# The opening of a one-core encoder step: first norm and first two products rearranged

## Chip, cores and metric

The kernel runs on one core of a Trainium2 chip. TensorE (PE) multiplies, VectorE (DVE), ScalarE (ACT) and GpSimd (POOL) do the elementwise work, SyncE (SP) issues most transfers. The metric is the device time of one launch in microseconds (us).

## The reference, cut to what matters

The reference is one layer of a streaming encoder for 1024 prompt rows and 8 times 16 sample rows, 1152 rows of 1024 values in all. Only its first lines touch the change:

```
h = rmsnorm(x, norm_attn)                  # x * rsqrt(mean(x*x) + eps) * g
hq, hf, hi, hg, dq, dk, dv, mq, gl = split(h @ w_in)
fg = lb + (1 - lb) * sigmoid(hf)           # lb from a softmax over two rows of logits
k = 1 - fg;  b = cumsum(log(fg)) in chunks # HGRN2 branch, 8 heads of 128
bias = rel_bias[t5_bucket(pos_k - pos_q)]  # for the attention branch that comes second
```

After the HGRN2 branch come differential attention, attention to memory, a merge and a ConvFFN. They stay as they were.

## The kernel before, in words

Every product is made exact in three parts. ACT rounds a 128x1024 weight block to a high part (`round_w`, line 113), POOL subtracts for the low part (`rest_w`, line 118), and PE runs high times high, high times low and low times high. A product of one weight block (128 output features, all 1152 rows) is 8 slices of the inner dimension times 3 column groups of 384 rows times 3 parts, 72 matmuls of 128x384. A *piece* is one column group of it, 24 matmuls (`gemm_piece`). Weight blocks land in two staging buffers by turns; a load waits until the block two before has its low part.

PSUM is used as two groups of four banks. `take`, `ready` and `freed` hand a group from PE to the engine that reads it and back by counting semaphores, in a fixed order of results.

Each phase is one block of five instruction streams, one for each engine. All engines meet at the end of a block: nothing of the next block starts before every stream of this one is through.

`norm_phase` (line 199) works over nine tiles of 128 rows. For a tile, ACT squares and sums (line 256), POOL makes the reciprocal root (lines 328 and 329), DVE scales the rows (line 298), PE transposes them in 8 transposes (line 340), DVE multiplies by the gain into `h_full` (line 313), ACT rounds to `h_hi_part` (line 274) and DVE subtracts for `h_lo_part` (line 304). The row tile `x_rows` has four places. Beside tiles 0 and 1 PE makes the relative bias rows of all eight heads, four at a time, in banks 2 and 3 of both groups (line 349), and ACT copies them out (line 266) and stores them. The low parts of the first two weight blocks (forget, query) come last on POOL.

`hgrn_phase` (line 394) opens with both first products, forget and query, in full (line 892). Its SP stream loads the next two weight blocks, two mask constants, 18 pieces of the bias tables and four more constants (lines 468 to 485), the last of them `hgrn_onorm`. DVE waits for all of these constants at line 628. It adds the masks to the bias tables (lines 631 and 634, `near` and `bs`), and SP stores the tables in eight transfers (lines 517 to 522) before it loads the gate weight of head 0 (line 492). Then DVE does `decays` (key, forget gate, scan of the logarithm, first differences, lines 663 to 651) and `opening` (line 702), and enters the loop over heads. In a head, PE computes the score matrices DIAG, L0, L1, then the transposes VT, then L2 and so on. In front of each of them it takes a PSUM group and runs one *rider*, a piece of a product that is wanted later. DVE frees the group after the scores have been masked (line 698) and the rider copied (line 700). The rider of DIAG needs the low part of the value weight, rounded by ACT at line 544. VT waits until the scores of L1 are masked (line 839).

Of the kernel before, what the change touches and what calls it, by code (L numbers as in the profile page):

```python
# [14 lines left out]
P = 128  # L15
# [53 lines left out]
class Program:  # L69
# [12 lines left out]
    def setup(self):  # L82
# [13 lines left out]
        self.consts, self.cb = self.sem("constants_in"), 0  # L96
        self.dve = Count(nc.vector, self.sem("dve_chain"))
# [101 lines left out]
def norm_phase(g):  # L199

    nc = g.nc
    ctx = ExitStack()
    NX = 4
    xr = g.sb("x_rows", [P, NX, D], ctx=ctx)
# [7 lines left out]
    landed = [g.sem(f"x_landed{n}") for n in range(NX)]  # L212
    consts_in, cb = g.consts, g.cb
    summed, rstd, scaled, h_hi, h_lo, lb_sub, lb_exp = (
        g.sem(n) for n in ("x_summed", "x_rstd_ready", "x_scaled", "h_hi", "h_lo", "lb_shifted",
                           "lb_exp"))
    base_s = g.sem("base_constants")
# [4 lines left out]
    g.brow_out = g.sem("bias_row_out")  # L222

# [4 lines left out]
    with nc.Block() as block:  # L228
        @block.sync
        def _(sp):  # L230
            sp.dma_start(xr[:, 0, :], x_rows(0)).then_inc(landed[0], 16)
            sp.dma_start(g.ident[:], g.c["ident"]).then_inc(consts_in, 16)
            with nc.allow_non_contiguous_dma(reason="columns of 1024 values"):
                sp.dma_start(gcol[:], columns(g.x["norm_attn"][0])).then_inc(consts_in, 16)
                for n in range(2):
                    sp.dma_start(lbl[:, n, :], columns(g.x["hgrn_lb_logits"][n])).then_inc(consts_in, 16)
            sp.dma_start(table[:], g.x["rel_bias"]).then_inc(bias_in, 16)
            sp.dma_start(hot[:], g.c["bucket_hot"]).then_inc(bias_in, 16)
            for t in range(1, NT):
                if t >= NX:  # L240
                    sp.wait_ge(g.full, g.r + t - NX + 1)
                sp.dma_start(xr[:, t % NX, :], x_rows(t)).then_inc(landed[t % NX], 16)
                if t == NX - 1:
                    g.load_w(sp, g.w_in(W_HF), 0)
                    g.load_w(sp, g.w_in(W_HQ), 1)

        @block.scalar
        def _(act):
            act.wait_ge(base_s, 3)
            act.wait_ge(lb_sub, 3)  # L250
            act.activation(lbl[:], lbl[:], ACT.Exp).then_inc(lb_exp, 1)
            def squares(t):
                act.wait_ge(landed[t % NX], 16 * (t // NX + 1))
                if t:
                    act.wait_ge(summed, t)
                act.activation(sq[:], xr[:, t % NX, :], ACT.Square, accum_out=ss[:, t:t + 1]).then_inc(summed, 1)
            squares(0)
            squares(1)
            for t in range(NT):
                if t + 2 < NT:  # L260
                    squares(t + 2)
                if t in (0, 1):
                    act.wait_ge(brow_full, t + 1)
                    for n in range(2):
# [9 lines left out]
                act.activation(g.hhi[:, :, t * P:(t + 1) * P], tmp[:, t % 2], ACT.Copy).then_inc(h_hi, 1)  # L274

        @block.vector
        def _(dve):
# [5 lines left out]
            dve.wait_ge(consts_in, cb + 64)  # L283
# [11 lines left out]
            def scale(t):  # L295
                v = rs[:, t:t + 1]
                dve.wait_ge(rstd, t + 1)
                dve.tensor_scalar(xr[:, t % NX, :], xr[:, t % NX, :], v, None, ALU.mult).then_inc(scaled, 1)

            def rest(t):  # L300

                dve.wait_ge(h_hi, t + 1)
                cols = slice(t * P, (t + 1) * P)
                dve.tensor_tensor(g.hlo[:, :, cols], tmp[:, t % 2], g.hhi[:, :, cols].bitcast(F32), ALU.subtract)\
                    .then_inc(h_lo, 1)
            scale(0)
            for t in range(NT):
                if t + 1 < NT:
                    scale(t + 1)
                if t >= 2:  # L310
                    dve.wait_ge(h_lo, t - 1)
                ps = g.ready(dve, t)
                g.freed(dve.tensor_tensor(tmp[:, t % 2], ps[:, 0:2, :].rearrange("p c (k n) -> p (c k) n", n=P),
                                          gcol[:].unsqueeze(2).to_broadcast([P, KT, P]), ALU.mult), t)
                if t:
                    rest(t - 1)
            rest(NT - 1)

        @block.gpsimd
        def _(pool):  # L320
            pool.wait_ge(base_s, 3)
            pool.wait_ge(bias_in, 32)
            pool.tensor_scalar(spread[:], table[:].unsqueeze(2).to_broadcast([BUCKETS, HEADS, P]), 1.0, None, ALU.mult)\
                .then_inc(base_s, 1)
# [5 lines left out]
            g.rest_w(pool, 0)  # L330
            g.rest_w(pool, 1)

        @block.tensor
        def _(pe):
            pe.wait_ge(consts_in, cb + 64)
            for t in range(NT):
                pe.wait_ge(scaled, t + 1)
                ps = g.take(pe, t)
                for k in range(KT):
                    last = pe.transpose(ps[:, k // 4, (k % 4) * P:(k % 4 + 1) * P],  # L340
                                        xr[:, t % NX, k * P:(k + 1) * P], g.ident[:])
                last.then_inc(g.full, 1)
                if t in (0, 1):
                    if t:
                        pe.wait_ge(brow_r, 2)
                    else:
                        pe.wait_ge(base_s, 4)
                    for n in range(4):
                        last = pe.matmul(g.psum[n // 2][:, 2 + n % 2, 0:NREL], spread[:, 4 * t + n, :], hot[:],
                                         start=True, stop=True)  # L350
                    last.then_inc(brow_full, 1)
    g.cb += 64
# [41 lines left out]
def hgrn_phase(g):  # L394
# [8 lines left out]
    g.first = ExitStack()  # L403
    g.first_q, g.first_k = (g.sb(n, [P, ROWS], ctx=g.first) for n in ("diff_q", "diff_k"))
# [22 lines left out]
     ns_r, sq_r, rt_r, y1_r, y_r, ln_r, zero_r) = (g.sem(n) for n in (  # L427
# [3 lines left out]
         "sample_states_new", "out_squares_ready", "out_rstd", "out_normed", "y0_ready", "out_log", "hgrn_zeroed"))  # L431
# [9 lines left out]
    pre = Results(g, ["F", "Q"])  # L441
    g.r += pre.n
# [22 lines left out]
    with nc.Block() as block:  # L465
        @block.sync
        def _(sp):
            g.load_w(sp, g.w_in(W_HI), W_VT)
            g.load_w(sp, g.w_in(W_HG), W_GS)
            sp.dma_start(chid, g.c["chunk_hidden"]).then_inc(consts_in, 16)  # L470
# [3 lines left out]
            sp.wait_ge(g.brow_out, 16)  # L474
# [56 lines left out]
        def _(act):  # L531
            act.wait_ge(zero_r, 1)
# [88 lines left out]
        def _(dve):  # L621
            dve.memset(sc[:], 0.0).then_inc(zero_r, 1)
# [132 lines left out]
            with dve.Fori(0, HEADS - 1) as i:  # L755
                head(i)
# [1922 lines left out]
```

## Time and profile before

| what | us |
|---|---|
| median of 3 runs | 3357.67 |
| lowest, highest | 3355.53, 3358.48 |
| the profiled execution's own time | 3354.4 |
| its span | 3352.6 |
| PE busy | 3149.6 (94%) |
| DVE, ACT, POOL busy | 1388.4, 1127.4, 872.6 |

The span runs from the first to the last instruction of the core. The profiled execution lies below the three timed runs, by 3.3 us against their median. Busy time of PE counts pipelined matmuls and does not say how fast they are; their spacing does.

### The profile page before, as it was taken

What the parts mean: (1) busy time and instruction counts of PE and PEld (TensorE: products, weight loads), DVE (VectorE), ACT (ScalarE), POOL (GpSimd) and SP (SyncE); (2) the same over time, 40 slices, a digit from 0 to 9 for tenths busy, and PEclk for the clock granted to TensorE, in tenths of its full rate; (3) what the DMA queues carried; (4) which work ended last, traced back from release to release, by engine and by line L of the source; (5) the groups of instructions that cost most, each with busy time, mean ns of one, the idle gap of its engine ahead of it and who ended that gap; (6) DMA issues with size and microseconds to landing.
All of it is one profiled execution on the core that took longest, in us unless ns stands there. A gap on an engine that the chain in (4) does not pass through costs nothing. (4 is left out here: it accounts for less than half of the span.)

```text
span 3352.6 us, 50047 instructions
## 1 busy us (share of the span) xinstructions
PE 3149.6 (94%) x19550; PEld 2963.1 (88%) x19550; DVE 1388.4 (41%) x1446; ACT 1127.4 (34%) x1586; POOL 872.6 (26%) x520
## 2 busy tenths in 40 slices
PE   6999999999999999999688888999979999999997
PEld 5899999999988888888477778999979999999996
DVE  5554354443525555555532322222044444444443
ACT  3344333433334444444332221112242222222222
POOL 2333233332312111212002121243343323222230
PEclk9999999999999999999799999999989999999998
DMA  5212121121258777877665536432211111111101
GB/s 158 70 40 72 52 59 56 49 72 52 59 105 149 120 134 139 158 131 146 124 132 141 122 101 215 142 108 73 79 38 57 38 44 44 38 44 38 38 25 68
DMA packets 684752, 295.69 MB, mean 88 GB/s; under 512 B 350524, under 2 KB 665436, under 8 KB 684680
## 3 DMA queue, kind: packets, MB, share of 16 engines
q1 hardware_dynamic: 680232, 285.90, 35.6%
q10 hardware_dynamic: 4448, 8.80, 0.7%
q8 instruction: 49, 0.80, 0.1%
q14 instruction: 23, 0.19, 0.0%
HBM read 240.23 MB, written 54.41 MB: 88 GB/s over the span
## 5 line engine op out<-in xcount | busy, mean ns | idle before, releaser
L118 POOL TENSOR_TENSOR weight_lo<-weight_stage,weight_hi 128x1024 fp32r<-128x1024 f32 x180 | 453.0, 2518 | 1480.5 <-ACT weight_hi L113 1480.5
L1862 PE MATMUL group<-act_hi_part,weight_hi 128*128 128x384 f32 x1056 | 360.8, 342 | 13.6 <-DVE act_lo_part L2091 9.3
L1863 PE MATMUL group<-act_lo_part,weight_hi 128*128 128x384 f32 x1056 | 359.8, 341 | 0.0
L1864 PE MATMUL group<-act_hi_part,weight_lo 128*128 128x384 f32 x1056 | 359.7, 341 | 0.0
L165 PE MATMUL group<-h_hi_part,weight_hi 128*128 128x384 f32 x936 | 332.9, 356 | 27.6 <-DVE key_rows L700 20.1
L113 ACT ACTIVATE weight_hi<-weight_stage 128x1024 fp32r<-128x1024 f32 x180 | 190.6, 1060 | 422.5 <-PE group L2133 231.9
L166 PE MATMUL group<-h_lo_part,weight_hi 128*128 128x384 f32 x936 | 318.8, 341 | 0.0
L167 PE MATMUL group<-h_hi_part,weight_lo 128*128 128x384 f32 x936 | 318.4, 340 | 0.0
L2131 PE MATMUL group<-act_hi_part,weight_hi 128*128 128x384 f32 x768 | 259.4, 338 | 12.1 <-DVE act_lo_part L2044 12.1
L2132 PE MATMUL group<-act_lo_part,weight_hi 128*128 128x384 f32 x768 | 258.6, 337 | 0.0
L2133 PE MATMUL group<-act_hi_part,weight_lo 128*128 128x384 f32 x768 | 258.5, 337 | 0.0
L1350 PE MATMUL group<-h_hi_part,weight_hi 128*128 128x384 f32 x696 | 244.0, 351 | 1.1 <-ACT next_v L1096 1.0
L1350 PE MATMUL group<-h_hi_part,weight_lo 128*128 128x384 f32 x696 | 237.8, 342 | 0.0
L1350 PE MATMUL group<-h_lo_part,weight_hi 128*128 128x384 f32 x696 | 235.9, 339 | 0.0
L698 DVE COPY_PREDICATED scores<-level_masks,group 128x1152 f32<-128x1152 uint32 (+2 forms) x88 | 91.8, 1073 | 308.8 <-PE group L823 307.7
L1862 PEld LDWEIGHTS group<-act_hi_part,weight_hi 128*128 128x128 f32 x1056 | 199.6, 189 | 17.1 <-issue 9.9
L165 PEld LDWEIGHTS group<-h_hi_part,weight_hi 128*128 128x128 f32 x936 | 179.5, 192 | 35.7 <-issue 20.5
L1863 PEld LDWEIGHTS group<-act_lo_part,weight_hi 128*128 128x128 f32 x1056 | 199.7, 189 | 0.0
L1864 PEld LDWEIGHTS group<-act_hi_part,weight_lo 128*128 128x128 f32 x1056 | 199.6, 189 | 0.0
L166 PEld LDWEIGHTS group<-h_lo_part,weight_hi 128*128 128x128 f32 x936 | 179.2, 191 | 4.3 <-issue 3.3
L167 PEld LDWEIGHTS group<-h_hi_part,weight_lo 128*128 128x128 f32 x936 | 179.1, 191 | 0.0
L2408 DVE TENSOR_TENSOR residual<-residual,group 128x1152 f32<-128x1152 f32 x80 | 108.4, 1354 | 163.2 <-PE group L2523 163.2
(348 smaller groups left out, 6691.3 us busy)
## 6 DMA issues: line engine op xcount, KB each, us to landing
weight_stage<-in_w_in SPq DMA_DIRECT2D x88, 512.0 KB, 4.8
cached_v<-in_cache_diff_v SPq DMA_DIRECT2D x128, 256.0 KB, 5.1
cached_k<-in_cache_diff_k SPq DMA_DIRECT2D x224, 128.0 KB, 4.3
weight_stage<-in_w_up SPq DMA_DIRECT2D x44, 512.0 KB, 3.9
y_stage<-scratch_y_branch SPq DMA_DIRECT2D x24, 576.0 KB, 9.4
gate_in<-scratch_gates SPq DMA_DIRECT2D x24, 576.0 KB, 3.8
weight_stage<-in_w_branch SPq DMA_DIRECT2D x24, 512.0 KB, 3.9
down_stage<-in_w_down SPq DMA_DIRECT2D x22, 512.0 KB, 3.6
```

The costliest lines, as they stand in the source:

```text
L113: act.activation(self.whi[:, n % 2, :], self.wst[:, n % 2, :], ACT.Copy).then_inc(self.w_hi, 1)
L118: pool.tensor_tensor(self.wlo[:, n % 2, :], self.wst[:, n % 2, :], self.whi[:, n % 2, :].bitcast(F32), ALU.subtract).then_inc(self.w_lo, 1)
L165: pe.matmul(out, wh[:, k, :], xh[:, k, cols], start=(k == 0), stop=False)
L166: pe.matmul(out, wh[:, k, :], xl[:, k, cols], start=False, stop=False)
L167: last = pe.matmul(out, wl[:, k, :], xh[:, k, cols], start=False, stop=(k == KT - 1))
L1350: ins = pe.matmul(rider_bank, w[:, k, :], x[:, k, c * CW:(c + 1) * CW], start=(at == 0), stop=(at == STEPS - 1))
L1862: pe.matmul(o, w[0][:, k, :], ahi[:, k, rows], start=(k == 0), stop=False)
L1863: pe.matmul(o, w[0][:, k, :], alo[:, k, rows], start=False, stop=False)
L1864: last = pe.matmul(o, w[1][:, k, :], ahi[:, k, rows], start=False, stop=(k == KT - 1))
L2131: pe.matmul(o, wh[:, k, :], ahi[:, k, cols], start=(k == 0 and open_sum), stop=False)
L2132: pe.matmul(o, wh[:, k, :], alo[:, k, cols], start=False, stop=False)
L2133: last = pe.matmul(o, wl[:, k, :], ahi[:, k, cols], start=False, stop=(k == KT - 1))
```

## The change

In the norm, every tile gets its own place in `x_rows`, so a load waits for a square sum and no more for a transposition. The lower bound of the forget gate is computed at the end instead of the beginning. Bias rows are made one head at a time, one matmul behind each tile from tile 2 on. POOL makes the low parts of tiles 1, 3, 5 and 7, DVE the others. The two first products are cut into six pieces; five of them are run by PE inside the norm's block, in bank 3 of each group: forget 0 behind tile 5, query 0 behind tile 7, then forget 1, query 1 and forget 2 after the last bias row. ACT copies each out (through the sigmoid for forget). The sixth, query 2, opens `hgrn_phase`. In that phase the wait for the stored bias rows moves in front of the two mask loads, and DVE adds the masks to the bias tables after `opening` and no more before `decays`. In `diff_phase` the rider semaphores are replaced by the two of the pieces, counted on; several semaphores of zeroed buffers are one.

```diff
 # norm_phase
-    NX = 4
-    xr = g.sb("x_rows", [P, NX, D], ctx=ctx)
+    xr = g.sb("x_rows", [P, NT, D], ctx=ctx)
+    g.piece_bank = [g.psum[n][:, 3, 0:CW] for n in range(2)]
+    pieces = [(p, c) for c in range(NC) for p in range(2)]
+    def bias_bank(h):
+        return g.psum[(g.r + h + 1) % 2][:, 2, 0:NREL]
 # sync: x0, ident, x1, norm_attn, x2, w(HF), x3, rel_bias, bucket_hot, w(HQ), x4..x8, lb_logits
+            def load_x(t):
+                if t >= 4:
+                    sp.wait_ge(summed, t - 3)
+                sp.dma_start(xr[:, t, :], x_rows(t)).then_inc(landed[t % 4], 16)
 # scalar
-            act.wait_ge(lb_sub, 3)
-            act.activation(lbl[:], lbl[:], ACT.Exp).then_inc(lb_exp, 1)
             squares(0)
             squares(1)
             for t in range(NT):
                 if t + 2 < NT:
                     squares(t + 2)
                 if t in (0, 1):
-                    act.wait_ge(brow_full, t + 1)
-                    for n in range(2):
-                        h = 4 * t + 2 * n
-                        act.activation(brow[:, h:h + 2, :], g.psum[n][:, 2:4, 0:NREL], ACT.Copy).then_inc(brow_r, 1)
-                if t == 1:
-                    act.wait_ge(brow_r, 4)
-                    act.dma_start(g.s["bias_row"].rearrange("h p n -> p h n"), brow[:]).then_inc(g.brow_out, 16)
-                if t == 3:
-                    g.round_w(act, 0)
-                    g.round_w(act, 1)
+                    g.round_w(act, t)
+                if t >= 3:
+                    bias_row(t - 3)
+                if t == 7:
+                    piece_out(0)
                 act.wait_ge(g.free[(g.r + t) % 2], (g.r + t) // 2 + 2)
                 act.activation(g.hhi[:, :, t * P:(t + 1) * P], tmp[:, t % 2], ACT.Copy).then_inc(h_hi, 1)
+            bias_row(HEADS - 2)
+            piece_out(1)
+            bias_row(HEADS - 1)
...
+            piece_out(2)
+            piece_out(3)
+            piece_out(4)
 # vector: rest(t) now for even t only; the lower bound's six operations after rest(NT - 1)
 # gpsimd
             for t in range(NT):
...
+                if t == 1:
+                    pool.wait_ge(bias_in, 32)
+                    pool.tensor_scalar(spread[:], ...)
+                if t in (2, 3):
+                    g.rest_w(pool, t - 2)
+                if t in (3, 5, 7):
+                    rest(t - 2)
+            rest(NT - 2)
 # tensor
+            def piece(k):
+                p, c = pieces[k]
+                w = g.w_parts(pe, p)
+                pe.wait_ge(h_lo[0], (2, 3, 5)[c])
+                pe.wait_ge(h_lo[1], (1, 3, 4)[c])
+                if c:
+                    pe.wait_ge(g.piece_out, k - 1)
+                g.gemm_piece(pe, g.piece_bank[p], w, (g.hhi, g.hlo), c).then_inc(g.piece_full, 1)
             for t in range(NT):
...
+                if 2 <= t:
+                    bias_row(t - 2)
+                if t == 5:
+                    piece(0)
+                if t == 7:
+                    piece(1)
+            bias_row(HEADS - 1)
+            piece(2)
+            piece(3)
+            piece(4)
 # hgrn_phase, sync
             g.load_w(sp, g.w_in(W_HI), W_VT)
             g.load_w(sp, g.w_in(W_HG), W_GS)
+            sp.wait_ge(g.brow_out, 16)
             sp.dma_start(chid, g.c["chunk_hidden"]).then_inc(consts_in, 16)
...
-            sp.wait_ge(g.brow_out, 16)
 # hgrn_phase, scalar
-            ps = pre.ready(act, "F")
-            pre.freed(act.activation(tiles(fg[:]), ps[:, 0:NC, 0:CW], ACT.Sigmoid), "F")
             act.wait_ge(fg_r, 1)
             act.activation(fg[:], fg[:], ACT.Ln).then_inc(logf_r, 1)
+            act.wait_ge(g.piece_full, 6)
+            act.activation(qq[:, 2 * CW:], g.piece_bank[1], ACT.Copy).then_inc(g.piece_out, 1)
             g.round_w(act, W_VT)
-            ps = pre.ready(act, "Q")
-            pre.freed(act.activation(tiles(qq[:]), ps[:, 0:NC, 0:CW], ACT.Copy), "Q")
 # hgrn_phase, vector
             dve.wait_ge(consts_in, cb + 96)
-            dve.wait_ge(near_in, NEAR_IN)
-            (the two and the four additions of masks to the bias tables)
...
             decays(0, 0)
             opening(0, 0)
+            dve.wait_ge(near_in, NEAR_IN)
+            (the same six additions)
 # hgrn_phase, tensor
-            for n, j in (("F", 0), ("Q", 1)):
-                w = g.w_parts(pe, j)
-                g.gemm_t(pe, pre.take(pe, n), w, (g.hhi, g.hlo)).then_inc(g.full, 1)
-            pre.wait_freed(pe, "Q")
+            w = g.w_parts(pe, 1)
+            pe.wait_ge(g.piece_out, 4)
+            g.gemm_piece(pe, g.piece_bank[1], w, (g.hhi, g.hlo), 2).then_inc(g.piece_full, 1)
+            pe.wait_ge(g.piece_out, 6)
```

## Rows read from the trace of the kernel before

**Rows 1.** Page, part 1: busy us (share of the span) of each engine.

```profile
PE 3149.6 (94%) x19550; PEld 2963.1 (88%) x19550; DVE 1388.4 (41%) x1446; ACT 1127.4 (34%) x1586; POOL 872.6 (26%) x520
```

**Rows 2.** Waits of SP's queue, first 130 us: total, times, longest.

```profile
SPq L228 <- PEq L228: 19.2, 1, 19.2
```

**Rows 3.** Timeline, PE in the norm: start, duration, instruction, idle before.

```profile
14.20 5.48 PE L349 MATMUL group<-bucket_hot,bias_table_spread 32*128 32x384 f32 x8
...
32.89 1.97 PE L340 MATMUL group<-ident,x_rows 128*128 128x128 f32 x8 [2.29 <-DVE x_rows L298]
...
35.82 1.97 PE L340 MATMUL group<-ident,x_rows 128*128 128x128 f32 x8 [0.96 <-DVE x_rows L298]
```

**Rows 4.** Timeline, ACT and POOL at the start of the norm.

```profile
7.11 1.28 ACT L251 ACT_TABLE_LOAD   x1 [7.11 <-DVE lb_logits L288]
...
7.67 2.77 POOL L323 TENSOR_SCALAR bias_table_spread<-bias_table 32x1024 f32<-32x1024 f32 x1 [7.23 <-DMA bucket_hot<-in_bucket_hot]
```

**Rows 5.** Timeline, DVE and POOL at the norm's end.

```profile
43.64 6.02 POOL L118 TENSOR_TENSOR weight_lo<-weight_stage,weight_hi 128x1024 fp32r<-128x1024 f32 x2
44.61 2.83 DVE L298 TENSOR_SCALAR x_rows<-x_rows,x_rstd 128x1024 f32<-128x1024 f32 x1
47.36 1.21 DVE L313 TENSOR_TENSOR h_full<-group,norm_attn_col 128x1024 f32<-128x1024 f32 x1
...
48.49 2.25 DVE L304 TENSOR_TENSOR h_lo_part<-h_full,h_hi_part 128x1024 fp32r<-128x1024 f32 x1
```

**Rows 6.** Timeline, POOL: a low part with no DVE work beside it.

```profile
139.19 2.35 POOL L118 TENSOR_TENSOR weight_lo<-weight_stage,weight_hi 128x1024 fp32r<-128x1024 f32 x1
```

**Rows 7.** Windows: length; busy (count) of PE, PEld, DVE, ACT, POOL; clock; DMA; GB/s.

```profile
54.80:59.40 4.60, 4.58 (x14) 4.60 (x15) 1.16 (x2) 0.00 (x0) 0.00 (x0) 1.00 0.80 226
59.40:80.00 20.60, 20.60 (x120) 20.60 (x120) 6.02 (x8) 3.70 (x3) 0.00 (x0) 1.00 0.67 175
```

**Rows 8.** Timeline, PE: riders of DIAG and L1, scores of L1, rider and transposes of VT.

```profile
86.85 0.69 PE L165 MATMUL group<-h_hi_part,weight_hi 128*128 128x384 f32 x1 [4.69 <-POOL weight_lo L118]
...
103.07 0.44 PE L165 MATMUL group<-h_hi_part,weight_hi 128*128 128x384 f32 x1 [2.09 <-DVE key_rows L700]
...
108.91 2.17 PE L823 MATMUL group<-mixed 128*128 128x128 f32 x18
...
113.36 0.44 PE L165 MATMUL group<-h_hi_part,weight_hi 128*128 128x384 f32 x1 [2.27 <-DVE key_rows L700]
...
119.20 1.15 PE L184 MATMUL group<-ident,key_rows 128*128 128x128 f32 x9
```

**Rows 9.** Timeline, SP from the barrier on, and DVE behind it.

```profile
54.63 1.00 SPq L107 DMA_DIRECT2D weight_stage<-in_w_in  x2
...
69.20 0.43 SPq L485 DMA_DIRECT2D hgrn_onorm<-in_hgrn_onorm  x1
...
73.77 2.49 DVE L631 TENSOR_TENSOR gate<-gate,out_squares 128x1024 f32<-128x1024 f32 x2 [17.66 <-DMA hgrn_onorm<-in_hgrn_onorm]
```

**Rows 10.** Timeline, DVE and ACT, from `decays` to the scores of L1.

```profile
79.08 0.87 DVE L663 TENSOR_SCALAR key<-diff_q,bound_less_one,one_less_bound 128x1152 f32<-128x1152 f32 x1
...
80.91 1.17 ACT L543 ACTIVATE diff_q<-diff_q 128x1152 f32<-128x1152 f32 x1 [7.42 <-DVE diff_q L665]
...
82.11 2.56 DVE L667 TENSOR_TENSOR_SCAN log_decay<-scan_keep,diff_q 128x1152 f32<-128x1152 f32 x1 [1.23 <-ACT diff_q L543]
...
103.16 1.46 DVE L698 COPY_PREDICATED scores<-level_masks,group 128x1152 f32<-128x1152 uint32 x1 [0.15 <-DVE key_rows L700]
...
104.97 0.75 DVE L678 TENSOR_TENSOR mixed<-decay,diff_k 128x576 f32<-128x576 f32 x1
...
111.33 1.46 DVE L698 COPY_PREDICATED scores<-level_masks,group 128x1152 f32<-128x1152 uint32 x1 [3.14 <-PE group L823]
```

**Rows 11.** Timeline, first table load behind the barrier, and SP behind the tables.

```profile
69.76 1.28 ACT L541 ACT_TABLE_LOAD   x1 [16.66 <-PE group L152]
...
88.14 9.29 SPq L107 DMA_DIRECT2D weight_stage<-in_w_in  x2
```

More of the change, by code:

```diff
@@ L282, in _, with scale, rest @@
             dve.sem_inc(g.free[1], 1)
-            dve.wait_ge(consts_in, cb + 64)
+            dve.wait_ge(consts_in, cb + 32)
+            def scale(t):
+                v = rs[:, t:t + 1]
+                dve.wait_ge(rstd, t + 1)
+                dve.tensor_scalar(xr[:, t, :], xr[:, t, :], v, None, ALU.mult).then_inc(scaled, 1)
+            def rest(t):
+                dve.wait_ge(h_hi, t + 1)
+                cols = slice(t * P, (t + 1) * P)
+                dve.tensor_tensor(g.hlo[:, :, cols], tmp[:, 0], g.hhi[:, :, cols].bitcast(F32), ALU.subtract)\
+                    .then_inc(h_lo[0], 1)
+            scale(0)
+            for t in range(NT):
+                if t + 1 < NT:
+                    scale(t + 1)
+                if t >= 2:
+                    dve.wait_ge(h_lo[t % 2], t // 2)
+                ps = g.ready(dve, t)
+                g.freed(dve.tensor_tensor(tmp[:, t % 2], ps[:, 0:2, :].rearrange("p c (k n) -> p (c k) n", n=P),
+                                          gcol[:].unsqueeze(2).to_broadcast([P, KT, P]), ALU.mult), t)
+                if t % 2:
+                    rest(t - 1)
+            rest(NT - 1)
+            dve.wait_ge(lb_in, 32)
             dve.tensor_tensor(lbm[:], lbl[:, 0, :], lbl[:, 1, :], ALU.max).then_inc(lb_sub, 1)
@@ L294, in _, with rest @@
             g.dve.done(dve.tensor_scalar(g.lb1n[:], g.lb1[:], -1.0, None, ALU.mult))
[L295 to L317, printed above, removed]
         @block.gpsimd
         def _(pool):
+            def rest(t):
+                pool.wait_ge(h_hi, t + 1)
+                cols = slice(t * P, (t + 1) * P)
+                pool.tensor_tensor(g.hlo[:, :, cols], tmp[:, 1], g.hhi[:, :, cols].bitcast(F32), ALU.subtract)\
+                    .then_inc(h_lo[1], 1)
             pool.wait_ge(base_s, 3)
-            pool.wait_ge(bias_in, 32)
-            pool.tensor_scalar(spread[:], table[:].unsqueeze(2).to_broadcast([BUCKETS, HEADS, P]), 1.0, None, ALU.mult)\
-                .then_inc(base_s, 1)
             for t in range(NT):
@@ L340, in _ @@
                     last = pe.transpose(ps[:, k // 4, (k % 4) * P:(k % 4 + 1) * P],
-                                        xr[:, t % NX, k * P:(k + 1) * P], g.ident[:])
+                                        xr[:, t, k * P:(k + 1) * P], g.ident[:])
                 last.then_inc(g.full, 1)
[L343 to L352, printed above, removed]
+                if 2 <= t:
[8 more added lines that the diff above has]
+            piece(4)
+    g.cb += 32
     g.r += NT
@@ L754, in _ @@
             opening(0, 0)
+            dve.wait_ge(near_in, NEAR_IN)
+            for n in range(2):
+                g.dve.done(dve.tensor_tensor(near[n], near[n], chid.unsqueeze(1).to_broadcast([P, 4, 2 * P]), ALU.add))
+            for n in range(2):
+                for k in range(2):
+                    ins = dve.tensor_tensor(
+                        bs[k][:, :, n, :].rearrange("p h (b s) -> p h b s", s=DEC_S),
+                        toep[:, 4 * k:4 * k + 4, :].unsqueeze(2).to_broadcast([P, 4, DEC_B, DEC_S]),
+                        shid[:, n, :].rearrange("p (b s) -> p b s", s=DEC_S).unsqueeze(1)
+                        .to_broadcast([P, 4, DEC_B, DEC_S]), ALU.add)
+                    if (n, k) == (1, 1):
+                        ins.then_inc(near_r, 1)
+                    else:
+                        g.dve.done(ins)
             with dve.Fori(0, HEADS - 1) as i:
@@ L1346, in ride @@
                         if at == 0:
-                            pe.wait_ge(rider_free, rider(piece, i, last) + 1)
+                            pe.wait_ge(g.piece_out, rider(piece, i, last))
                         k, part = divmod(at, 3)
```

119 lines of the change are left out of this document (62 added, 57 removed).

## The prediction

> **What bounds the kernel now.** I read the page's first part, then the waits and the timelines of the first 130 us, since nothing behind them changes. PE is busy for 94% of the span [rows 1], so over the whole kernel a microsecond by which the heads' loop starts later is a microsecond at the end. The opening is different: there PE waits for others. The waits show SP standing 19.2 us at a block's border [rows 2]: engines that are through with the norm wait until all are. The border is passed at 54.63, when SP issues its next loads [rows 9]. Behind it PE runs 144 matmuls of the two first products, the first 14 at 0.33 us each and the next 120 at 0.172 [rows 7]. Meanwhile DVE waits 17.7 us for the last of 24 transfers that SP could issue only after the border: 54.63 to 73.77 [rows 9]. From 73.77 the end is set by DVE, not by PE: masks on the bias tables until 79.08, then `decays` and `opening` until about 103 [rows 10]. PE stands still for 4.7 us before the rider of DIAG, and 2.1 and 2.3 us before those of L1 and VT, each time behind DVE or what DVE holds up [rows 8]. After the scores of L1 PE leads again: its next matmul, the rider of VT, starts at 113.36 [rows 8]. I call this point S. The prediction is where S goes, and what happens to the border on the way.
>
> **Part 1: from the border B to S.** Before, S is B + 58.7 (113.36 less 54.63). After, the chain is:
> - B to the last constant: SP issues the same transfers in the same order; the wait for the stored bias rows is only moved up by two small loads, and their store is issued about 12 us ahead of B. 19.1 us.
> - `decays` may start at once, since the masks come later: key and gate, 79.08 to 80.91 [rows 10], 1.8 us.
> - The logarithm is now ACT's first operation behind the border. The first one of a stage has its table load behind its waits (7.11, and 69.76) [rows 4, 11]. 1.3 us, or 0 if the load slips in front of the wait. I take 1.3, since both first operations show it.
> - Logarithm, 1.2 us; from the scan's start at 82.11 to the point where the scores of L0 begin at 103.16, 21.05 us [rows 10]. ACT rounds the value weight behind this logarithm, as before, so POOL's low part holds up DVE's differences again at the same place.
> - The masks on the tables, now here: 73.77 to 79.08, 5.3 us [rows 9, 10].
> - Scores of L0 until DVE is ready for L1: 103.16 to 108.19 (111.33 less 3.14), 5.0 us. Scores of L1 until S, 111.33 to 113.36, 2.0 us [rows 8, 10].
>
> Sum 56.8 us. PE's own branch is shorter: it may start the rider of L1 at B + 44.4 and needs 8.0 us to the end of the L1 matrices (103.07 to 111.08) [rows 8], so B + 52.4, while DVE comes to the scores of L1 at B + 54.8. So the moved masks cost 2.4 us of path, not 5.3, and 1.9 us are saved against 58.7. That is all that can be won behind the border. PE, freed of five sixths of its products there, waits: query 2 is done at about B + 5, and the low part of the value weight, rounded behind the logarithm, comes 4.7 us after the scan's start (86.85 less 82.11), at B + 28. Some 23 us of PE stand empty. Bounds of this part: 55.5 (no table load) to 57.5.
>
> **Part 2: where the border goes.** First the norm up to piece 0. The first square no longer waits for the lower bound. With some 5 us for the first tile to land, table load, square, root and scaling, the first transposes start near 9. Then POOL and DVE get in each other's way. At 44.61 a scaling took 2.83 us while POOL made a low part; it ended 0.8 us after the first of POOL's two must have ended. The low part at 48.49 took 2.25 and ended 1.1 after POOL's second. `h_full`, which reads PSUM, took its 1.21 beside POOL [rows 5]. So I count scalings (0.75) and DVE's low parts (1.1) as excluded while POOL runs a large operation. Before the transposes of tile 5, that adds up to: spreading the table 2.8 [rows 4], two weight and two tile low parts on POOL at 2.35 [rows 6], five scalings, and two low parts on DVE: 2.8 + 9.4 + 3.75 + 2.2 = 18.1 us. Laid one behind the other from 9.3, with some 3.5 us in which this port is idle because the next user waits for a transposition, `h_full` or the rounding, the transposes of tiles 1 to 5 start at 12.8, 16.0, 21.5, 25.5 and 31.1. With their 2 us and a bias row of 1.3 (5.48 for what four heads take, two records each, so 1.28) [rows 3], piece 0 starts at 34. Without any exclusion the same layout gives 28.8; with tiles a little later, 36.
>
> The Trainium skill says the same against this change: GPSIMD Engine Reference, section 2, Architecture, has GpSimd's SBUF port shared with VectorE, and its section 1 names operations with two SBUF inputs, or in a two-port mode, as those that contend. Had they not contended, the forecast below would be 5.4 us less, by the layout's 28.8; rows 5 agree with the page.
>
> From there PE alone sets the pace, as an in-order engine with everything else ready:
> - Piece 0, cold: 10 to 14 matmuls at 0.33, the rest at 0.172 [rows 7], and the cold riders took 5.8 (103.07 to 108.91) [rows 8]. 5.6 to 6.2, taken 6.0.
> - Tiles 6 and 7 with two bias rows: at the half clock 2 x 1.88 + 2 x 1.28 = 6.3 [rows 3]; at the full one a transpose takes half (9 in 1.15) [rows 8], 3.2. The norm's transposes and bias rows never reached the full clock before, so they may drop it again. Taken 4.3.
> - Piece 1: 4.15 (24 x 0.172) to 6.2, taken 5.2. Tile 8 and two bias rows: 2.3 to 4.4, taken 3.0. Piece 2: 4.15 to 6.2, taken 5.2. Pieces 3 and 4: 4.15 each.
>
> Sum 32.0 us (27.7 to 37.6). Piece 4 ends at 66.2. Its copy by ACT and the border itself take 1.0 us. B = 67.2, against 54.63: the norm's block is 12.6 us longer. Bounds 28.8 + 27.7 + 1 = 57.5 and 36 + 37.6 + 1 = 74.6.
>
> **The sum.** S after is 67.2 + 56.8 = 124.0, against 113.36: 10.6 us later. Behind S the order and the work are the same, and PE leads, so the end moves by 10.6. The profiled execution took 3354.4; 3365.0 by it. The median of the runs shown lies 3.3 above, so 3368.3 for the median, and all times below are in its terms. With the bounds of both parts: 57.5 + 55.5 - 113.4 = -0.4, so 3357; 74.6 + 57.5 - 113.4 = 18.7, so 3376. What the edit moves is 20.6 us of products from behind the border, where DVE's wait of 19.1 us covered them, to before it, where they delay those very transfers.
>
> **Edits at nothing.** The counters of `diff_phase` and the joined semaphore wait for the same events. Nine places for `x_rows`: the loads no longer wait for transposes, but from tile 2 on the squares are ahead of the scalings anyway. The lower bound at the end: ten small operations while PE has three pieces to run; if these were gone it would show with some 3 us.
>
> **Rivals.**
> *A: the norm and the clock go well, no measurable change.* Little contention and a full clock through tiles 6 to 8: B near 60, S 3 us later, 3361. For it: the cover of the second product may keep PE at full speed. Against: 8 transposes in 1.97 and bias rows at 1.28 throughout the norm. I give 0.17.
> *B: PE's gaps swallow the pieces, faster.* The bias rows of tiles 0 and 1 kept PE 5.5 us each [rows 3]; undisturbed tiles come every 2.9 us (32.89 to 35.82) [rows 3]. If all tiles ran so, tile 5 would be through at 26, and if the first three pieces only filled waiting time between tiles, the norm's last tile would be done near 40 and two pieces, 8.3 us, would follow: B = 50, S = 50 + 55.5 = 105.5, 7.9 us earlier, 3350. It decides from B below 50. Against: PE is in order, so piece 0 stands in front of tile 6; 27.7 us of PE must follow tile 5 in any case. 0.05.
> *C: forecast, and the tables come late as well.* The masks end at S - 7, SP needs 88.14 less 79.08, 9.1 us, before it loads the gate weight [rows 10, 11], and that lands about 4.6 later (69.20 to 73.77) [rows 9]. It is there at S + 7. ACT stands at its rounding in front of the copy of VT; that copy would end at S + 11, and PE needs the bank at S + 13. If the load took 4 us more, PE would stand 2 to 3 us: 3371. 0.15.
>
> **How the numbers follow.** The forecast has 0.63, C 0.15, A 0.17, B 0.05. Of the forecast's own spread (3361 to 3376) a tenth lies within 0.2% of before. 0.2% (6.7 us) is about what a measurement can tell from no change. Slower by more: 0.63 + 0.15 less 0.05, 0.73. Within: 0.17 and 0.05, 0.22. Faster: 0.05. The range reaches from A's 3359 to 3376.
>
> **What would show it.** Right: SP's first transfer behind the norm near 67 instead of 54.6; DVE's wait for `hgrn_onorm` still ending 19 us behind it; PE idle for over 20 us in front of the first value piece; scalings of 2 to 3 us beside POOL's low parts; S near 124. Wrong: a border before 58; a DVE that starts `decays` sooner than 19 us after it; or a loop whose distance from S to the end shrinks.

## The result, and the profile after

| kernel | median us | lowest, highest | runs |
|---|---|---|---|
| before | 3355.53 | 3350.12, 3358.48 | 5 |
| after | 3368.95 | 3364.78, 3368.98 | 5 |

The ratio is 1.0041, with a 95% interval of 1.0029 to 1.0052: the change makes the kernel slower by 13.4 us. The forecast was 3368. That it lies within 1 us of the median is in part luck: it added 10.6 us to a median of 3357.67 for the kernel before, which came out at 3355.53 here, and the shift was larger than forecast. The profiled execution of after took 3368.91, its span is 3367.1.

The page of after, part 1 [rows 1]: the same work, so nothing was added that could explain 13 us.

```profile
PE 3144.5 (93%) x19550; PEld 2959.4 (88%) x19550; DVE 1389.2 (41%) x1442; ACT 1129.9 (34%) x1596; POOL 882.5 (26%) x524
```

The timeline of SP: the transfers at the start, the first issue behind the border, and the last constant [rows 9].

```profile
4.07 2.82 SPq L243 DMA_DIRECT2D x_rows<-in_x_prompt  x1
...
7.41 0.42 SPq L254 DMA_DIRECT2D bucket_hot<-in_bucket_hot  x1
...
68.42 0.99 SPq L108 DMA_DIRECT2D weight_stage<-in_w_in  x2
...
81.96 0.43 SPq L537 DMA_DIRECT2D hgrn_onorm<-in_hgrn_onorm  x1
```

The waits of SP in the first 130 us [rows 2]: 44.3 us at the border, where it stood 19.2. Of the 25.1 us more, 13.8 are the later border; the rest is SP being through with its loads earlier (last issue at 22.84, before at 34.89).

```profile
SPq L237 <- PEq L237: 44.3, 1, 44.3
```

The timeline of DVE in the norm, and then from the border to the scores of L1 [rows 5, 10]. The masks on the tables are now the L792 row, behind the opening.

```profile
16.36 2.83 DVE L316 TENSOR_SCALAR x_rows<-x_rows,x_rstd 128x1024 f32<-128x1024 f32 x1 [4.14 <-POOL x_rstd L361]
...
31.22 2.83 DVE L316 TENSOR_SCALAR x_rows<-x_rows,x_rstd 128x1024 f32<-128x1024 f32 x1 [0.71 <-POOL x_rstd L361]
...
87.78 0.88 DVE L698 TENSOR_SCALAR key<-diff_q,bound_less_one,one_less_bound 128x1152 f32<-128x1152 f32 x1 [17.89 <-DMA hgrn_onorm<-in_hgrn_onorm]
...
92.14 2.56 DVE L702 TENSOR_TENSOR_SCAN log_decay<-scan_keep,diff_q 128x1152 f32<-128x1152 f32 x1 [2.57 <-ACT diff_q L593]
...
112.95 2.47 DVE L792 TENSOR_TENSOR gate<-gate,out_squares 128x1024 f32<-128x1024 f32 x2
...
118.24 1.44 DVE L733 COPY_PREDICATED scores<-level_masks,group 128x1152 f32<-128x1152 uint32 x1
...
123.17 1.44 DVE L733 COPY_PREDICATED scores<-level_masks,group 128x1152 f32<-128x1152 uint32 x1
```

The timeline of POOL: spreading the table, and one of its four low parts of tiles [rows 4, 6].

```profile
12.65 2.77 POOL L364 TENSOR_SCALAR bias_table_spread<-bias_table 32x1024 f32<-32x1024 f32 x1 [3.06 <-DMA bucket_hot<-in_bucket_hot]
...
31.15 2.34 POOL L354 TENSOR_TENSOR h_lo_part<-h_full,h_hi_part 128x1024 fp32r<-128x1024 f32 x1
```

The timeline of PE: tile 5 and a bias row, piece 0, then tiles and bias rows between pieces, the rider of DIAG, the scores of L1, and the rider of VT [rows 3, 8].

```profile
34.10 1.97 PE L395 MATMUL group<-ident,x_rows 128*128 128x128 f32 x8 [1.01 <-DVE x_rows L316]
36.01 1.64 PE L379 MATMUL group<-bucket_hot,bias_table_spread 32*128 32x384 f32 x2
37.58 0.69 PE L166 MATMUL group<-h_hi_part,weight_hi 128*128 128x384 f32 x1
...
44.47 1.04 PE L395 MATMUL group<-ident,x_rows 128*128 128x128 f32 x8
45.44 0.91 PE L379 MATMUL group<-bucket_hot,bias_table_spread 32*128 32x384 f32 x2
...
48.14 0.45 PE L166 MATMUL group<-h_hi_part,weight_hi 128*128 128x384 f32 x1
...
96.88 0.69 PE L166 MATMUL group<-h_hi_part,weight_hi 128*128 128x384 f32 x1 [23.86 <-POOL weight_lo L119]
...
117.35 2.17 PE L872 MATMUL group<-mixed 128*128 128x128 f32 x18
...
125.18 0.68 PE L166 MATMUL group<-h_hi_part,weight_hi 128*128 128x384 f32 x1 [5.66 <-DVE key_rows L735]
```

Read together: the border moved from 54.63 to 68.42 (+13.8). Behind it DVE waits for the same last constant as before, 17.9 us against 17.7. S moved from 113.36 to 125.18 (+11.8). The transposes and bias rows between the pieces run at nearly twice the speed they had before piece 0 (1.04 against 1.97, 0.91 against 1.64). Windows of both stretches, with the columns of rows 7, have PE at the lower of its two clock levels (0.50, 1.2 GHz) in the first and at the upper one (1.00, 2.4 GHz) in the second:

```profile
26.00:37.50 11.50, 10.41 (x30) 6.20 (x30) 10.11 (x10) 7.12 (x12) 5.83 (x8) 0.50 0.04 0
43.40:54.80 11.40, 11.40 (x63) 8.99 (x62) 5.44 (x5) 4.54 (x6) 2.38 (x1) 1.00 0.01 1
```

In the trace of the kernel before, the clock column reads 1.00 also where matmuls are 0.33 us apart [rows 7]; there only the spacing shows the half speed.

### The profile page after: what moved, and what is told of

The parts are those of the page before. It is cut to its first block and busy times, and to the rows that moved or that the text cites. A ratio compares the mean times of both kernels' runs of the same rounds, so it can differ in the third digit from the quotient of the medians.

```text
span 3367.1 us, 50051 instructions
## 1 busy us (share of the span) xinstructions
PE 3144.5 (93%) x19550; PEld 2959.4 (88%) x19550; DVE 1389.2 (41%) x1442; ACT 1129.9 (34%) x1596; POOL 882.5 (26%) x524
## 5 line engine op out<-in xcount | busy, mean ns | idle before, releaser
L166 PE MATMUL group<-h_hi_part,weight_hi 128*128 128x384 f32 x984 | 351.7, 357 | 51.2 <-POOL weight_lo L119 23.9
L168 PE MATMUL group<-h_hi_part,weight_lo 128*128 128x384 f32 x984 | 337.0, 342 | 0.0
L167 PE MATMUL group<-h_lo_part,weight_hi 128*128 128x384 f32 x984 | 336.9, 342 | 0.0
L166 PEld LDWEIGHTS group<-h_hi_part,weight_hi 128*128 128x128 f32 x984 | 190.2, 193 | 61.7 <-issue 27.4
L1397 PE MATMUL group<-h_hi_part,weight_hi 128*128 128x384 f32 x696 | 243.5, 350 | 1.1 <-ACT next_v L1144 1.0
L1397 PE MATMUL group<-h_hi_part,weight_lo 128*128 128x384 f32 x696 | 237.5, 341 | 0.0
L1397 PE MATMUL group<-h_lo_part,weight_hi 128*128 128x384 f32 x696 | 235.4, 338 | 0.0
L167 PEld LDWEIGHTS group<-h_lo_part,weight_hi 128*128 128x128 f32 x984 | 190.1, 193 | 4.3 <-issue 3.3
L168 PEld LDWEIGHTS group<-h_hi_part,weight_lo 128*128 128x128 f32 x984 | 189.6, 193 | 0.0
```

The source lines that it names most:

```text
L166: pe.matmul(out, wh[:, k, :], xh[:, k, cols], start=(k == 0), stop=False)
L167: pe.matmul(out, wh[:, k, :], xl[:, k, cols], start=False, stop=False)
L168: last = pe.matmul(out, wl[:, k, :], xh[:, k, cols], start=False, stop=(k == KT - 1))
L1397: ins = pe.matmul(rider_bank, w[:, k, :], x[:, k, c * CW:(c + 1) * CW], start=(at == 0), stop=(at == STEPS - 1))
```

## The experiments

Each was timed in turn with the kernel before on its own chip, so ratios are compared across kernels and not medians. Diffs are against the changed kernel, except where they say against before. In the expectations T is my theory: the end is set by the border, then by the wait for the last constant and DVE's chain. R1: what costs is PE standing empty and cold before the value weight. R2: what costs is POOL and DVE holding each other up in the norm.

### All six pieces behind the border

```
-                if t == 5:
-                    piece(0)
-                if t == 7:
-                    piece(1)
...
-            piece(2)
-            piece(3)
-            piece(4)
...
+            for k in range(0, 6):          # in hgrn_phase, in front of the heads
+                ...gemm_piece(pe, g.piece_bank[k % 2], w, (g.hhi, g.hlo), c)
```

The pieces go in the order forget 0 to 2, query 0 to 2; ACT's copies move with them.

> The changed kernel with all six pieces behind the border (forget first, then query), everything else of the change kept. Theory T (the end is the border plus the wait for the last constant plus DVE's chain): the border falls from 68.4 to about 54, now set by the lower bound's small operations at the norm's end, since no piece runs after tile 8. The pieces again lie beside the wait for the constants. S = 54 + 56.8 = 111, some 14 us earlier than the 125.2 of the changed kernel; time 3354 to 3356, so level with the kernel before. Rival R1 (what costs is PE standing empty before the value weight and starting cold): gives the same sign, but S relative to the border falls as well, below 50. Rival R2 (POOL's low parts and the one-by-one bias rows stretched the norm): the border stays above 60.

Measured: 3357.07, ratio 1.001 (1.0001 to 1.0019), S 112.46. The timelines of SP and DVE:

```profile
53.23 1.89 SPq L108 DMA_DIRECT2D weight_stage<-in_w_in  x2
...
70.09 0.57 SPq L524 DMA_DIRECT2D hgrn_onorm<-in_hgrn_onorm  x1
```

```profile
75.32 0.88 DVE L695 TENSOR_SCALAR key<-diff_q,bound_less_one,one_less_bound 128x1152 f32<-128x1152 f32 x1 [20.62 <-DMA hgrn_onorm<-in_hgrn_onorm]
```

The border is back where it was, and with it 0.31% of the 0.41%, or 10 us. The rest, 3.4 us by the ratio, lies between 0.3 and 6.4 by its interval and is not explained: S is 0.9 us earlier than in the kernel before. So the pieces in front of the border carry most of the loss. The norm's other rearrangements together are worth 1.4 us of border (53.23 against 54.63). R1 expected S less than 50 us behind the border and R2 a border above 60; S lies 59.2 us behind a border at 53.2, so both fall. The wait for the transfers was 3 us longer this time, 22.1 us from border to `decays`, and S came 1.5 us later than I expected.

### The six constants first

```
             sp.wait_ge(g.brow_out, 16)
+            (scan_keep, level_masks, stream_rows, hgrn_onorm)
             (chunk_hidden, stream_hidden)
             (the 18 table loads)
-            (scan_keep, level_masks, stream_rows, hgrn_onorm)
```

> The changed kernel with one edit: SP issues the six constants that DVE waits for ahead of the 18 loads of the bias tables. T: the border stays at 68.4, DVE starts decays about 10 us behind it instead of 19.4, everything of DVE's chain follows, S near 115.7, time near 3359.5. R1: PE's empty stretch only gets shorter at its end and S stays where PE's work puts it, no change (3369). R2: no change.

Measured: 3359.31, ratio 1.0018 (1.001 to 1.0027). The timelines of SP and DVE:

```profile
67.65 0.99 SPq L108 DMA_DIRECT2D weight_stage<-in_w_in  x2
...
71.10 0.68 SPq L527 DMA_DIRECT2D hgrn_onorm<-in_hgrn_onorm  x1
```

```profile
78.16 0.88 DVE L698 TENSOR_SCALAR key<-diff_q,bound_less_one,one_less_bound 128x1152 f32<-128x1152 f32 x1 [9.04 <-DMA out_squares<-in_stream_hidden]
```

`decays` now starts 10.5 us behind the border instead of 19.4, and S is 115.96, where 115.7 was expected. Of the 9.2 us by which S is earlier, 0.8 are this run's earlier border (67.65); the other 8.4 (S less border 48.3, against 56.8) came back by the order of SP's queue. So the wait behind the border is a second, separate term, as T says.

### The value weight rounded before the logarithm

```
+            g.round_w(act, W_VT)
             act.wait_ge(fg_r, 1)
             act.activation(fg[:], fg[:], ACT.Ln).then_inc(logf_r, 1)
...
-            g.round_w(act, W_VT)
```

> The changed kernel with ACT rounding the value weight before the logarithm instead of behind it, so that PE can run the rider of DIAG some 10 us behind the border and its 24 us of standing still are broken up. T: only the port is freed, POOL's low part no longer lies in front of DVE's first difference, 2 us; time 3367. R1: 15 us or more come back, 3354.

Measured: 3365.08, ratio 1.0036 (1.0023 to 1.0049). The timelines of DVE and PE:

```profile
87.32 3.00 DVE L698 TENSOR_SCALAR key<-diff_q,bound_less_one,one_less_bound 128x1152 f32<-128x1152 f32 x1 [17.05 <-DMA hgrn_onorm<-in_hgrn_onorm]
```

```profile
93.15 0.68 PE L166 MATMUL group<-h_hi_part,weight_hi 128*128 128x384 f32 x1 [19.75 <-ACT diff_k L596]
...
123.51 0.68 PE L166 MATMUL group<-h_hi_part,weight_hi 128*128 128x384 f32 x1 [4.10 <-DVE key_rows L735]
```

The weight is ready earlier, but PE still stands 19.8 us (in-order, its first rider waits for the copy of query 2 by ACT), and S is 123.51, 1.7 us earlier. I had expected the rider of DIAG some 10 us behind the border; it starts 24.3 us behind it. A part of what was won is paid at once: POOL's low part now lies beside `key`, which takes 3.00 instead of 0.88. The expectation of R1, 3354, is not met. But as a test of R1 this run is weak, since most of PE's stop remained, and in time it cannot be told from the changed kernel. What speaks against R1 is the first experiment: there PE stood for 5.1 us and not 23.9 before that rider, and the way from the start of `decays` to S still took 37.1 us, against 37.4 in the changed kernel.

### All low parts of tiles on DVE

```
-                dve.tensor_tensor(g.hlo[:, :, cols], tmp[:, 0], ...ALU.subtract).then_inc(h_lo[0], 1)
+                dve.tensor_tensor(g.hlo[:, :, cols], tmp[:, t % 2], ...ALU.subtract).then_inc(h_lo[t % 2], 1)
...
-                if t in (3, 5, 7):         # POOL
-                    rest(t - 2)
-            rest(NT - 2)
```

> The changed kernel with all nine low parts on DVE again, as before the change; pieces and bias rows stay. T: piece 0 starts some 2.5 us earlier (35 instead of 37.6), the rest is PE's, border near 66, time near 3366.5. R2 (the stretch of the norm's block is contention between POOL and DVE): the border comes back to 55 to 58 and the time to 3356.

Measured: 3364.0, ratio 1.0035 (1.0021 to 1.0048); border 64.98, S 121.25. The timelines of DVE and PE:

```profile
16.30 2.82 DVE L316 TENSOR_SCALAR x_rows<-x_rows,x_rstd 128x1024 f32<-128x1024 f32 x1 [4.06 <-POOL x_rstd L355]
...
29.00 0.74 DVE L316 TENSOR_SCALAR x_rows<-x_rows,x_rstd 128x1024 f32<-128x1024 f32 x1
29.66 1.21 DVE L331 TENSOR_TENSOR h_full<-group,norm_attn_col 128x1024 f32<-128x1024 f32 x1
30.79 1.21 DVE L322 TENSOR_TENSOR h_lo_part<-h_full,h_hi_part 128x1024 fp32r<-128x1024 f32 x1
```

```profile
34.35 0.69 PE L166 MATMUL group<-h_hi_part,weight_hi 128*128 128x384 f32 x1
```

Without POOL's low parts scalings are back at 0.74, and a tile takes DVE 2.9 us. Piece 0 starts 3.2 us earlier, the border comes 3.4 us earlier. So R2 holds for 3.4 of the border's 13.8 us, and not for the rest: R2 expected 3356. In time the run cannot be told from the changed kernel, since the intervals of both ratios overlap.

### The masks before `decays` again

```
-            decays(0, 0)
-            opening(0, 0)
             dve.wait_ge(near_in, NEAR_IN)
             (masks on near and bs)
+            decays(0, 0)
+            opening(0, 0)
```

> The changed kernel with the masks on the bias tables ahead of decays again. My sum says that the masks cost 2.4 us at their new place and 5.3 at the old: T: S 2.9 to 3.5 us later (128.1 to 128.7 against 125.2), 3372. Rival: the place makes no difference, because PE or the gate weight leads behind the opening: 3369.

Measured: 3371.36, ratio 1.0046 (1.0032 to 1.006). The timeline of PE:

```profile
116.91 0.44 PE L166 MATMUL group<-h_hi_part,weight_hi 128*128 128x384 f32 x1 [1.23 <-DVE key_rows L735]
...
121.17 2.17 PE L872 MATMUL group<-mixed 128*128 128x128 f32 x18
...
125.61 0.44 PE L166 MATMUL group<-h_hi_part,weight_hi 128*128 128x384 f32 x1 [2.26 <-DVE key_rows L735]
```

The border was 67.52 here, so S came 58.1 behind it, against 56.8 after. The masks' new place is worth 1.3 us, not 2.9 to 3.5. The missing 1.6 is in the rows: the rider of L1 took 4.3 us to the scores (116.91 to 121.17), while in the kernel before it took 5.8 (103.07 to 108.91) [rows 8], ten of its matmuls at half speed. PE had stood for 1.23 us in front of it here, and for 2.09 us there. In time the intervals of both ratios overlap, so only the sign of the shift in S is shown, not a difference of medians.

### Against before: the masks behind the opening, then the constants first as well

```
+            decays(0, 0)                   # against before
+            opening(0, 0)
             dve.wait_ge(near_in, NEAR_IN)
             (masks on near and bs)
-            decays(0, 0)
-            opening(0, 0)
```

> The kernel before with one part of the change alone: DVE adds the masks to the bias tables after opening instead of before decays. Theory T: decays start at 73.8 instead of 79.1 us, but ACT copies the query product out only at 83 to 84, so the exponentials are held up; with 2.4 us of the masks still on the path behind, S near 111.5 instead of 113.36; time about 2 us under that of the kernel before. Rival: the masks cost as much in the new place (5.3 us between the scores of DIAG and L0, and tables and gate weight late), no change or slower.

> The same, and the six constants ahead of the 18 table loads. T: DVE's wait is no longer for transfers but for the forget product (its sigmoid ends at 72.2), and soon for the query product, done at 82 us, so little more comes: S near 110, time 3 to 4 us under the kernel before. Rival (transfers alone set the opening): 11 us under it, 3342.

Measured: 3354.95, ratio 0.9995 (0.9986 to 1.0003), for the masks alone; 3356.18, ratio 0.9999 (0.999 to 1.0008), with the constants first as in the second experiment. Neither can be told from before. The timeline of ACT in the second kernel:

```profile
70.21 1.13 ACT L541 ACTIVATE diff_q<-group 128x1152 f32<-128x1152 f32 x1
...
81.35 1.13 ACT L546 ACTIVATE diff_k<-group 128x1152 f32<-128x1152 f32 x1 [5.95 <-PE group L152]
82.50 1.28 ACT L537 ACT_TABLE_LOAD   x1
83.79 0.73 ACT L537 ACTIVATE decay<-decay 128x576 f32<-128x576 f32 x1
```

S is 110.98 with the masks alone, 2.4 us earlier than in the kernel before and near the 111.5 of theory T; no gain in time is shown. In the second kernel the constants are in time and `decays` starts at 71.45 (79.08 before), but it is now held by the forget product's sigmoid, which needs PE until 70.21. The exponentials stand behind the copy of query at 81.35, which needs the second product. S moved by 2.5 us only (110.86), nearly all of it by the masks: the order of the constants added 0.1. So in the kernel before, two limits lie close together: the last constant, and the 144 matmuls of products behind the border, which end only when ACT can copy at 81.35. In the kernel with the masks alone the same copy stands at 81.49.

### Constants first and two forget pieces inside

Pieces 0 and 1 of forget stay inside the norm; forget 2 and all of query go behind the border; constants first.

> The changed kernel with the constants first, and only two forget pieces inside the norm's block (behind tiles 5 and 7); the third and the three query pieces run behind the border beside the transfers. T: border near 60, decays at 70, held up 3 us by the copy of the last query piece in front of the first exponentials; S near 108, time near 3351.5, a little under the kernel before. Rival (pieces inside are free where PE waits anyway): the same as constants first alone, 3359.

Measured: 3354.83, ratio 0.9995 (0.9986 to 1.0004). Border 60.03, `decays` 70.00, S 110.67, 2.7 us later than expected. No gain that can be measured: the border is 6.8 us later than in the kernel with all six pieces behind it (53.23). The rival's 3359 falls too, so pieces inside are not free.

### One forget piece inside, constants first, low parts on DVE

On top of the last: one piece inside, behind the last bias row; DVE makes all low parts; the value weight is rounded before the logarithm; ACT does the first two exponentials before the copy of the last query piece.

```
+            piece_out(1)
+            piece_out(2)
+            g.round_w(act, W_VT)
+            piece_out(3)
             act.wait_ge(fg_r, 1)
             act.activation(fg[:], fg[:], ACT.Ln).then_inc(logf_r, 1)
+            piece_out(4)
             level(0, 0)
+            piece_out(5)
             level(1, 0)
```

> What the runs so far point to: constants first, all low parts on DVE, one forget piece inside behind the last bias row, five pieces behind the border, value weight rounded before the logarithm, first exponentials before the copy of the last query piece. T: border near 52, the last query piece done and copied near 75.5, from there 25.6 us of DVE's chain to S near 101; time near 3345, 8 to 9 us under the kernel before. Rival (the queue of small waits on ACT eats it): level with the kernel before.

Measured: 3343.89 (3342.99 to 3346.09, 5 runs), ratio 0.9966 (0.9953 to 0.9979). It beats both kernels. The timelines of SP and DVE:

```profile
53.81 0.99 SPq L108 DMA_DIRECT2D weight_stage<-in_w_in  x2
...
57.18 0.43 SPq L507 DMA_DIRECT2D hgrn_onorm<-in_hgrn_onorm  x1
```

```profile
64.36 3.05 DVE L687 TENSOR_SCALAR key<-diff_q,bound_less_one,one_less_bound 128x1152 f32<-128x1152 f32 x1 [9.08 <-DMA out_squares<-in_stream_hidden]
...
69.61 2.56 DVE L691 TENSOR_TENSOR_SCAN log_decay<-scan_keep,diff_q 128x1152 f32<-128x1152 f32 x1 [1.29 <-ACT diff_q L583]
```

S is 101.79, 11.6 us before that of the kernel before. The border is where it was; the chain behind it is shorter: S less border is 48.0, against 58.7 in the kernel before. What the single parts are worth on this kernel was tested for the order of the constants alone, in the next run.

### The same with the constants last

> The kernel called best with one thing taken back: the six constants behind the 18 table loads, as in the changed kernel. T: the border stays at 53.8; the last constant lands some 19 us behind it, not 3.4, so decays starts at 73.8, no longer at 64.4; without POOL's low part beside it key takes 0.9 and the scan starts near 78; then 32.2 us from scan to S as in best: S 110, 8 us later than best (101.8), so 3352. Rival: the gain of best comes from the shorter norm and the early value weight alone, and the order of the loads gives under 3 us: 3344 to 3347.

Measured: 3352.27, ratio 0.9989 (0.998 to 0.9998). The timelines of DVE and PE:

```profile
72.16 3.04 DVE L687 TENSOR_SCALAR key<-diff_q,bound_less_one,one_less_bound 128x1152 f32<-128x1152 f32 x1 [17.89 <-DMA hgrn_onorm<-in_hgrn_onorm]
```

```profile
109.47 0.68 PE L166 MATMUL group<-h_hi_part,weight_hi 128*128 128x384 f32 x1 [5.77 <-DVE key_rows L724]
```

S is 109.47, 7.7 us later than with the constants first, from a border 1.0 us earlier (52.80, where I expected 53.8), so 8.7 us lie behind the border. The ratios differ by 0.23%, also 7.7 us. `key` takes 3.04 and not the 0.9 of my expectation, because POOL waits for the same constants and makes its low part beside it, at 72.20. The parts need each other: the constants first, on top of before with the masks late, gave nothing that can be measured; everything else without them 0.1%; all together 0.34%.

## Why the prediction was right

The term of each step, as forecast and as measured:

| step | forecast | measured |
|---|---|---|
| piece 0 starts | 34 | 37.58 |
| PE from there to the end of piece 4 | 32.0 | 30.1 |
| last copy and border | 1.0 | 0.8 |
| border B | 67.2 | 68.42 |
| B to `decays` | 19.1 | 19.36 |
| `decays` to scan | 4.3 | 4.36 |
| masks, at their new place | 5.3 | 5.3 |
| B to S | 56.8 | 56.76 |
| shift of S | 10.6 | 11.8 |
| shift of the span | 10.6 | 14.5 |

**The norm up to piece 0 was 3.6 us too short in my sum.** That POOL and DVE exclude each other was right (scalings of 2.83 at 16.36 and 31.22 beside POOL's subtractions), and the experiment with all low parts on DVE gives the price of POOL's four, 3.2 us at piece 0. What I had not counted is a transfer. The bias table for the spreading is issued at 7.41, behind a load of a row tile whose issue took SP 2.82 us, and POOL spreads at 12.65; before, it spread at 7.67 [rows 4]. I had counted the changed order of loads in the norm at nothing. The next scaling, at 16.36, waits 4.1 us behind it, and the transposes of tile 2 start at 19.24, where my layout had 16.0. That this lateness reaches piece 0 is read from the timelines; no run takes it back. Another 0.3 us is the bias row behind tile 5, 1.57 (36.01 to 37.58) where I took 1.28.

**PE's part was 1.9 us shorter.** Piece 0 was slower than taken (6.9, not 6.0), but then PE never fell back: tiles 6 and 7 with their bias rows took 3.7 (taken 4.3, bounds 3.2 and 6.3), piece 1 4.3 (5.2), tile 8 2.45 (3.0). Behind piece 0 the lower bounds were nearly right. Piece 0 itself lay outside its bounds of 5.6 to 6.2: seventeen of its matmuls ran at half speed, where I had 10 to 14. The two errors of this sum, 3.6 too short and 1.9 too long, cancel in part in B. That is luck; B is 1.2 us later than forecast.

**From the border to S every term held.** The first operation of ACT behind the border has its table load behind its wait, as taken:

```profile
89.65 1.28 ACT L593 ACT_TABLE_LOAD   x1 [21.50 <-DVE diff_q L700]
```

The masks' net price against their old place was off: I had 2.4 us of path instead of 5.3, and the experiment that puts them back shows a gain of 1.3 us rather than 2.9, because PE's rider of L1, which bounds the old order, ran 1.6 us faster there than in the trace of before.

**Rival A** needed a border near 60 and falls, though half of it came true: PE kept full speed through tiles 6 to 8. The contention did not stay small. **Rival B** needed one below 50 and falls: PE is in order, and 30.1 us followed tile 5. **Rival C**'s late tables did occur. The gate weight is rounded at 133.32, 8.1 us behind S (I had it landing at S + 7), and ACT stood 10 us for it. The copy of VT at 135.33 was in time all the same, so C's extra 3 us did not arise:

```profile
133.32 1.06 ACT L114 ACTIVATE weight_hi<-weight_stage 128x1024 fp32r<-128x1024 f32 x1 [10.01 <-DMA weight_stage<-in_w_in]
...
135.33 1.11 ACT L618 ACTIVATE value_rows<-group 128x1152 f32<-128x1152 f32 x1
```

**Behind S** the span lost 2.7 us more than S. My text took the rest as equal; the windows of single heads show equal work at another clock for most of it. Two neighbouring heads of after, with the columns of rows 7:

```profile
143.53:251.32 107.79, 105.28 (x664) 103.09 (x663) 49.16 (x50) 40.57 (x46) 33.06 (x16) 0.98 0.19 57
251.32:357.49 106.17, 103.66 (x664) 101.47 (x663) 49.20 (x50) 40.58 (x46) 33.11 (x16) 1.00 0.19 57
```

Of the seven steps from head to head, two take 107.8 and five 106.1 in after; in the kernel before one takes 107.65. In each of these three one rider, after a stop of PE of 2.27 or 2.28 us, took 5.84 us and not 4.27 (at 232.98 and 765.49, and at 539.44 in before), and that is the whole difference. One such step more is 1.6 us of the 2.7; another 0.5 is spread over the seven steps, and 0.6 lies behind the heads, which I did not trace. Such single slow steps may also be part of the spread among one kernel's runs (3350.12 to 3358.48 for before), in which 2.5 us of S can't be seen; that was not tested.

The Trainium skill says, in GPSIMD Engine Reference, section 2, Architecture, that GpSimd has one read and one write port into SBUF and shares both with VectorE. The traces agree for operations on SBUF alone: 2.83 against 0.74 for a scaling, 3.00 against 0.88 for `key`. They also show that not every DVE operation is held up: `h_full`, which reads PSUM and writes SBUF, took 1.21 with POOL beside it [rows 5] and without.

## What to carry to other kernels

Work that is moved in front of a border between blocks, where all engines meet, delays every transfer that is issued behind it, and if it used to cover those very transfers, it can cost nearly its whole length: the five pieces, 23.9 us of PE, put the border 15.2 us later than it is with all six behind it (68.42 against 53.23), and no run shows that they shortened the path behind it. Ask first what is waited for behind the border, and order the queue by first need: six small constants ahead of 18 table loads brought S 8.4 us nearer to the border in one kernel and 8.7 in another without moving any work. Then look for the next limit before counting the gain, since the same order gave 0.1 us of S and nothing measurable where the products bound the same point.

## What the runs showed of the hardware

- In the changed kernel PE kept full speed between two product pieces through 8 transposes of 128x128 and bias rows of 32 rows (1.04 and 0.91 us, granted clock 1.00 from 43.40 to 54.80). The same instructions ran at half speed throughout the 28 us before the first piece (1.97 and 1.64), even where they ran with a single gap of 1.0 us, from 26.08 to 37.58 (granted clock 0.50).
- A rider of 24 matmuls takes 4.3 us at full speed and 5.8 with ten of them at half speed. How long PE had stood before it goes with this. In the first 1000 us of the twelve traces, none of 106 riders and pieces was slow that came after a stop of 0.15 to 1.55 us; of 87 after a stop of 2.09 to 2.29 us, 19 were; and all 24 were that came after 3.0 us or more. In before the rider of L1 was slow after 2.09 us [rows 8], in the kernel with the masks put back it was fast after 1.23 us.
- The table of buckets was waited for until 12.65 although it was issued at 7.41; issued 2.2 us earlier, at 5.25 before, it was there at 7.67. So it came 5.0 us later for an issue 2.2 us later. Four row tiles and a weight block are ahead of it in after, and of these large transfers only one row tile in before; that these cost the other 2.8 us is my reading and was not tested.
